# Two gates of the first merge among the last steps of the latent attention, a third ahead of the first branch product, and the splits of the branches' outputs later

## What is computed

```python
o_rwkv = _rwkv7_mix(p_rwkv, ...)
o_mla = _mla_mix(p_mla, ...)          # 8 heads, causal softmax over blocks of 128 queries
o_diff = _diff_mix(p_diff, ...)       # ends in an RMS norm over each head of 128
gates = jax.nn.sigmoid(p_gate + b_gate[l]).reshape(B, S, N_BRANCHES, D_MODEL)
merged = (gates[:, :, 0] * (o_rwkv @ w_branch_rwkv[l])
          + gates[:, :, 1] * (o_mla @ w_branch_mla[l])
          + gates[:, :, 2] * (o_diff @ w_branch_diff[l]))
x = x + merged @ w_o[l]
```

## Time and profile before

| | |
|---|---|
| Median of 3 runs | 3469.41 us (3463.99 to 3471.94) |
| Span of the profiled execution | 3464.9 us; no other time is given for that execution |
| Busy: PE, PEld, DVE, ACT, POOL | 3340.3, 2696.5, 1814.4, 1294.8, 116.1 us |
| Chain that ended last | PE 86%, DVE 8%, ACT 4% |
| Mean granted TensorE clock | 0.989 of full speed |
| End of the latent attention's last matmuls | 547.15 us |
| First merge | from there to about 754 us |

### The profile page before, as it was taken

How to read it: one execution, slowest core, us unless ns; L and a number is a source line. 1 busy time by engine, 2 the same in 40 slices (tenths; PEclk the granted TensorE clock), 3 DMA queues, 4 the chain that set the end, 5 groups by cost and what they waited for, 6 DMA issues and landing times.

```text
span 3464.9 us, 46862 instructions
## 1 busy us (share of the span) xinstructions
PE 3340.3 (96%) x19963; PEld 2696.5 (78%) x19963; DVE 1814.4 (52%) x3053; ACT 1294.8 (37%) x2160; POOL 116.1 (3%) x210
## 2 busy tenths in 40 slices
PE   7999989999999999999899999999999989999998
PEld 5878756888888888887568888888888756788887
DVE  5565664577656665654754533353334475453333
ACT  4232565335434422234543322332223354342222
POOL 0000000010000010100000000000000000000000
PEclk9999999999999999999999999999999999999999
DMA  3110013464444265643112222322333311223231
GB/s 139 39 50 24 31 43 110 161 220 142 153 157 151 90 241 195 244 139 101 32 55 86 97 96 94 98 92 98 97 98 112 105 38 49 86 85 97 98 97 67
DMA packets 100544, 364.08 MB, mean 105 GB/s; under 512 B 11632, under 2 KB 11696, under 8 KB 99696
## 3 DMA queue, kind: packets, MB, share of 16 engines
q1 hardware_dynamic: 75888, 272.14, 23.6%
q0 software_dynamic: 24448, 88.95, 7.8%
HBM read 358.94 MB, written 2.10 MB: 104 GB/s over the span
## 4 chain that ended last, share of the span: by engine, by line
PE 86%; DVE 8%; ACT 4%; issue 1%; DMA 0%; POOL 0%; DVEq 0%; ACTq 0%; POOLq 0%
PE ps_run L435 85%; PE ps_run L781 1%; DVE wl L1890 1%; DVE nrm L1897 1%; ACT nrm L1171 1%; DVE HL L1897 1%; ACT wh L1171 1%; ACT nP L1171 0%; DVE nst L2565 0%; DVE ug L1890 0%; DVE AL L1890 0%; DMA vec<-vec 0%; ACT HH L1171 0%; DVE dP L2258 0%; DVE nrm L1890 0%
## 5 line engine op out<-in xcount | busy, mean ns | idle before, releaser
L435 PE MATMUL ps_run<-HH,wh 128*128 128x512 f32 (+1 forms) x2720 | 1064.8, 391 | 17.8 <-DVE wl L1890 10.5
L435 PE MATMUL ps_run<-HH,wl 128*128 128x512 f32 (+1 forms) x2720 | 1038.4, 382 | 0.0
L435 PE MATMUL ps_run<-HL,wh 128*128 128x512 f32 (+1 forms) x2720 | 1037.8, 382 | 0.0
L1890 DVE TENSOR_TENSOR wl<-st,wh 128x1024 fp32r<-128x1024 f32 x511 | 624.9, 1224 | 733.9 <-ACT wh L1171 733.8
L1171 ACT ACTIVATE wh<-st 128x1024 fp32r<-128x1024 f32 x511 | 537.3, 1054 | 708.4 <-PE ps_run L435 703.4
L435 PEld LDWEIGHTS ps_run<-HH,wh 128*128 128x128 f32 x2720 | 512.9, 189 | 127.5 <-DVE wl L1890 8.5
L435 PEld LDWEIGHTS ps_run<-HL,wh 128*128 128x128 f32 x2720 | 513.5, 189 | 100.0 <-issue 5.5
L435 PEld LDWEIGHTS ps_run<-HH,wl 128*128 128x128 f32 x2720 | 512.8, 189 | 100.1
L435 PE MATMUL ps_run<-AH,wh 128*128 128x512 f32 (+1 forms) x1167 | 443.6, 380 | 2.1 <-DVE wl L1890 2.1
L435 PE MATMUL ps_run<-AH,wl 128*128 128x512 f32 (+1 forms) x1167 | 441.2, 378 | 0.0
L435 PE MATMUL ps_run<-AL,wh 128*128 128x512 f32 (+1 forms) x1167 | 441.2, 378 | 0.0
(11 more groups left out here) (408 smaller groups left out, 3344.2 us busy)
## 6 DMA issues: line engine op xcount, KB each, us to landing
st<-wst SPq DMA_DIRECT2D x511, 512.0 KB, 3.3
mb<-ada POOLq DMA_DIRECT2D x144, 512.0 KB, 4.4
cw<-cw POOLq DMA_DIRECT2D x4, 1024.0 KB, 7.0
X<-xT SPq DMA_DIRECT2D x8, 256.0 KB, 10.2
X<-xT POOLq DMA_DIRECT2D x8, 256.0 KB, 5.1
out<-X SPq DMA_DIRECT2D x8, 256.0 KB, 2.8
kc<-kc POOLq DMA_DIRECT2D x1, 1139.5 KB, 7.4
mb<-cond POOLq DMA_DIRECT2D x2, 512.0 KB, 5.1
```

What stands on the lines that cost most here:

```text
L435: i = self.e.matmul(out, lhsT, rhs, start=start, stop=stop, skip_group_check=True)
L1890: self.e.tensor_tensor(out, a, b, op).then_inc(*self.w.done(*points))
```

## The change

PE: gates 0 and 1 are cut into four pieces each of six matmuls, and two pieces stand behind the work of each of the steps 15, 16, 17 and 18 of the latent attention. Then come gate 2, branch products 0, 1 and 2, and from round 3 on gate and branch product as before.

ACT and DVE: the split that belongs to the first eight blocks stands ahead of the wait for the latent attention. Of the eight splits of branch outputs, four come first. ACT makes the other four in round 1, DVE one in each of the rounds 1 to 4. ACT's Silu moves into round 5. The list `fill` is not touched in rounds 0 to 5, and gives two steps in rounds 6 to 11, one in 12 to 15 and two from 16 on; that is 32 steps, as before.

```diff
-        finish(pipeline(16, (values, both(turn), scores), (4, 3, 0)))
+        ahead = chained(self.first_gate(0, 0), self.first_gate(0, 1))
+        for step, _ in enumerate(pipeline(16, (values, both(turn), scores), (4, 3, 0))):
+            if step >= 15:
+                next(ahead, None)
+                next(ahead, None)
+        finish(ahead)
...
-        gate(*order[0])
-        gate(*order[1])
+        gate(*order[2])
         branch(*order[0])
         branch(*order[1])
-        for this in order[2:]:
+        branch(*order[2])
+        for this in order[3:]:
             gate(*this)
             branch(*this)
...
         order = m.o[0:4] + m.o[8:12] + m.o[4:8]
+        finish(self.spend(8))
         w.wait_ge("dve mla")
         w.wait_ge("pe mla")
         w.own()
-        for j in range(8):
+        for j in range(4):
             self.half(("o", j), order[j], m.AH[j])
-        self.modulation(0)
         for br in range(3):
             for i in range(8):
-                finish(self.spend(8))
                 k = 8 * br + i
+                if k:
+                    finish(self.spend(8))
+                if k == 1:
+                    for j in range(4, 8):
+                        self.half(("o", j), order[j], m.AH[j])
+                if k == 5:
+                    self.modulation(0)
                 w.wait_ge("gate", br, i)
...
+        finish(self.spend(8))
         w.wait_ge("mla out")
         w.wait_ge("pe mla")
-        for j in range(8):
+        for j in range(4):
             self.rest(("o", j), order[j], m.AH[j], m.AL[j])
...
+                if k:
+                    finish(self.spend(8))
                 finish(self.spend(4))
+                if 1 <= k <= 4:
+                    self.rest(("o", 3 + k), order[3 + k], m.AH[3 + k], m.AL[3 + k])
...
-                for _ in range(2 if br == 2 else 1):
+                for _ in range(0 if k < 6 else 1 if 12 <= k < 16 else 2):
                     next(fill, None)
```

More of the change, by code:

```diff
@@ L896, in values, with first_gate @@
                             kt == 0, kt == i, *([("mO", n)] if kt == i else []))
-        finish(pipeline(16, (values, both(turn), scores), (4, 3, 0)))
+        ahead = chained(self.first_gate(0, 0), self.first_gate(0, 1))
[4 more added lines that the diff above has]
+        finish(ahead)
+    def first_gate(self, br, i):
+        m = self.m
+        base = 1792 + 416 + 1536
+        return self.linear(("gate", br, i), fe(c128(base + br * 1024 + i * 128), "w_in", (0,), 8), m.HH, m.HL, None, (0, 1, 2, 3))
     def merge_first(self):
         m = self.m
-        base = 1792 + 416 + 1536
         dense = (0, 1, 2, 3)
@@ L906, in gate @@
         def gate(br, i):
-            finish(self.linear(("gate", br, i), fe(c128(base + br * 1024 + i * 128), "w_in", (0,), 8), m.HH, m.HL, None, dense))
+            finish(self.first_gate(br, i))
         def branch(br, i):
```

## The result

| | us, median (lowest to highest) | runs |
|---|---|---|
| before | 3468.89 (3463.66 to 3472.75) | 20 |
| changed | 3475.14 (3469.90 to 3479.54) | 20 |

The ratio is 1.0019, with a 95% interval of 1.0013 to 1.0025: some 6.6 us slower, between 4.5 and 8.7. The forecast was 1.5 us faster, and the measured time lies above the range that was given. The difference is just under the 0.2% named at the start, but with 20 runs on each side the interval excludes no change. The profiled execution took 3476.05 us, with a span of 3474.1.

A forecast was written before the change was run, and what follows sets the result against it. PE, busy for 96% of the span, was taken as the bound. The terms 9.1 + 2.2 - 3.0 - 3.75 - 0.3 - 2.7 gave +1.5 us gained, so 3469.4 became 3467.9 us, range 3461.5 to 3474.5.

The forecast's parts named there:

- three waits: New PE waits: 3.0 us ahead of gate 2, 3.75 ahead of gate 3, 2.7 at round 5's `dsum`; clock holding.
- rival (3): The clock falls in all three new waits: 8.1 us slower, 3477.5 us; decided at gate 2; chance 0.05.
- Silu term: Round 5: the condition's load and two table loads delay the sigmoid, so PE waits 2.7 us more at `dsum`.
- rival (2): Clock falls in one new wait, likeliest the middle one: 1.6 us or up to twice that, 3470.3 us; chance 0.20.
- The tail: End of the latent attention: gate matmuls between its steps leave no wait and keep the clock up, gaining 9.1 us.
- Rival (4): Clock falls anyway in the latent attention's last steps: sum +9.4 us, 3478.8 us; chance 0.03.
- Slab 3: Old 2.2 us wait at branch product 0 goes; new 3.0 us wait at gate 2; slab 4 just 0.4 us early.
- The bank of gate 3: Gate 3 takes gate 2's bank and waits for that gate's sigmoid: a new PE wait of 3.75 us.
- The marker's sum: Start of gate 3's second half: 4.2 us earlier, from 9.1 + 2.2 - 3.0 - 3.75 less three times 0.1.
- The table loads: On ACT: each costs 1.28 us with the next instruction right behind it, without the 1.38 us drain.
- rival (6): ACT table switches cost up to twice 1.28 us: 1.6 us slower in sum, 3471.0 us; chance 0.02.
- What was moved at no cost: DVE's low parts 4 to 7, the moved `fill` steps and POOL's later `ada` loads cause no new wait.

The follow-up runs named there:

- experiment 3: Changed kernel with ACT splitting slab 3 after step 17 of the latent attention, ahead of the last output's copy; 3473.6 us, ratio 1.0013 to the kernel before.
- Experiment 8: Changed kernel with POOL issuing the three `ada` loads only after the Silu's end; 3475.99 us in one profiled run.
- experiment 4: Changed kernel with gate 2's product in the free bank 6, so gate 3 finds its bank empty; 3469.33 us, ratio 1.0000 to the kernel before.
- experiment 1: Changed kernel with 44 matmuls whose results nobody reads put into PE's three new waits; 3469.02 us, ratio 0.9999 to the kernel before.
- experiment 2: Changed kernel with the Silu in round 9 instead of 5 and `fill` from round 10; 3470.35 us, ratio 1.0002 to the kernel before.
- experiment 5: Changed kernel with gate 2 in bank 6 and the Silu in round 9; 3463.65 us, ratio 0.9983 to the kernel before.
- experiment 6: Changed kernel with gate 2 in bank 6, Silu in round 9, slabs 3 and 4 split in steps 17 and 18; 3461.09 us, ratio 0.9973 to before.

## Why the prediction was wrong

**The clock: the step that failed.** The forecast priced three waits and let the clock hold over each. Its evidence was one row, the wait of 3.02 us ahead of 1183.39 over which it held. It fell behind all three, so the sum lacked a term of 6.1 us: 1.6 behind gate 2, 1.6 behind gate 3, 2.9 behind `dsum` of round 5. The case was there as rival (3), with 0.05. That rival came nearest, 8.1 us slower where 6.6 were measured, but partly by luck: it priced the three falls at 9.6 us instead of 6.1, and its Silu term was 1.9 too small. For the first two falls the lower end of rival (2), 8 matmuls at twice their time, is the right size. Rival (3) also said that it would be decided at gate 2. The falls came together here, but not for that reason: in experiment 3 none comes at gate 2, and the other two come all the same.

The trace of the kernel before held more than that row. In the latent attention the clock was down as soon as PE started again behind a wait of 1.89 us, ahead of 537.75. At two later places with like instructions PE waited 2.8 us, once the clock held and once it fell about 1 us after the restart. PE's timeline of the kernel before at these two places:

```profile
1668.10 1.13 PE L435 MATMUL ps_run<-kw,qT 64*128 64x512 f32 x4 [2.81 <-ACT nP L1171]
...
2809.28 1.13 PE L435 MATMUL ps_run<-kw,qT 64*128 64x512 f32 x4 [2.80 <-ACT nP L1171]
```

And its windows behind the three waits:

```profile
537.00:538.00 1.00, 0.24 (x3) 0.28 (x5) 0.75 (x3) 0.61 (x3) 0.00 (x0) 0.50 0.00 0
1668.10:1672.10 4.00, 4.00 (x28) 2.53 (x29) 3.48 (x10) 3.95 (x7) 0.00 (x0) 1.00 0.30 111
2810.50:2811.50 1.00, 1.00 (x4) 0.81 (x3) 0.82 (x2) 0.98 (x2) 0.00 (x0) 0.50 0.00 0
```

Of the eleven waits of 1.8 to 4.4 us that PE has in that trace (the first, at the kernel's start, left out), seven had the clock at the lower level within 2 us of the restart. Counted like that, a fall behind at least one of the three new waits was the likely case, and not one of 0.25, which rivals (2) and (3) have together.

The rule of the Trainium skill that was weighed against that row, page "TensorE: Matmul & The Clock Gate", section "HAM oscillation — how this bites in real kernels", says that bursts of work with waits between them are throttled again for each burst; its example has waits of some 3 to 5 us. At the three new waits the trace agrees, 3 times in 3. I put it below a single row of the trace. But that row shows one outcome of an event that can go either way. The same wait, 3.01 to 3.03 us long, stands in all ten profiles of this study at the same place. The next 24 matmuls take, from start to start of gate matmuls:

| us | profiles |
|---|---|
| 5.6, the clock held | before, slab 3 early, gate 2 in bank 6, `ada` held |
| 7.1 to 7.2 | Silu in round 9, Silu and bank, before with Silu in round 9 |
| 8.3 to 8.4 | changed, waits filled, Silu bank and slabs |

It held in 4 of 10. Two rows of the changed kernel's timeline of PE, for which the kernel before has 1183.39 and 1188.97:

```profile
1188.08 0.79 PE L435 MATMUL ps_run<-HH,wh 128*128 128x512 f32 x1 [3.03 <-DVE wl L1905]
...
1196.45 0.39 PE L435 MATMUL ps_run<-HH,wh 128*128 128x512 f32 x1
```

That alone puts 2.8 of the 9.2 us between the spans of the two profiles shown. It is most likely chance and no effect of the change, though this can't be told from one profile of each kernel. One and the same kernel does vary that way: in 33 runs of the kernel before, its mean granted clock lies between 0.985 and 0.990, and the two runs at 0.985 took 3471.8 and 3471.9 us, the two at 0.990 3464.1 and 3465.7.

**The Silu: the term that was too small.** The forecast had it start 4.75 us behind POOL's load, which is what the old place showed, and kept 3.5 us as the upper bound for the wait "if POOL's load met more traffic". It started 6.55 us behind (599.31 less 592.76), and D2 came 4.6 us later instead of 2.7. Experiment 8 finds 1.5 of these 1.9: the three loads issued behind it. In the old place the same three loads stood behind it too, and yet it landed in 4.7. That stretch was clear of SP's loads of weights. In experiment 8 SP's loads were there and the three were not, and it took 5.0. So it looks as if both together made it slow; the new place without SP's loads was not tried. The rest of the term is right: two tables and the Silu follow as counted, and `dsum` starts 2.68 us behind the sigmoid, as before (2.69).

**What was right.**
- The tail. Clock 1.00 in all windows from 533.6 to 547.2, no wait in it, and the last values end 19.06 us behind T (548.26 and 1.09, less 530.29), where the forecast's 550.7 less 532.14 is 18.6. Rival (4) is out.
- Slab 3: 2.93 us for 3.0. Experiment 3 shows that slab 4 stood right behind it, as said.
- The bank of gate 3: 3.54 us for 3.75; experiment 4 shows the cause.
- The marker's sum, with the clock up: 4.17 for 4.3 (experiment 1). Changed as it was, T to G3 gained 2.61, since the fall behind gate 2 took 1.6 of it.
- The table loads. The sigmoid at 554.56 starts 0.01 us behind the end of the load of 1.28, and so does the one at 601.68 within 0.02. The drain that the Trainium skill gives, page "ScalarE: Activation LUTs", section "What ACT_TABLE_LOAD costs", isn't there; rival (6) is out.
- What was moved at no cost. D1 to D3 has its old length to 0.02 us as soon as the Silu is out of round 5 (experiments 2, 5, 6), so the low parts and the late `ada` loads cost nothing there. Behind `dsum` of round 5 the changed kernel's PE waits for nothing up to 800, so its `fill` didn't either.

**The sum as it came.** The forecast's +1.5, less 1.9 for the Silu, less 6.1 for the clock, gives 6.5 us slower. The profiles show 6.56, the runs 6.6, with 2 us to either side. That it meets to 0.1 is in part luck, as the terms for the tail, slab 3 and the bank were each off by 0.1 to 0.5.

## What to carry to other kernels

A wait of PE of about 3 us has two prices: its length, and 1.5 to 2.9 us lost in slow work behind it, which it may or may not draw. Count how often such a wait drew it over several profiles before you take one row as proof, and put the chance on the fall. A change that makes one stretch denser but leaves several new short waits behind it loses by them; look for their causes one by one (a bank reused too soon, a split queued behind the last output, a load issued just before it is needed), since each was a few lines' edit here and all of them together turned +0.19% into -0.27%. And try the smallest piece by itself: the Silu moved in the kernel before gave -0.14%, half of that.

## What the runs showed that I had not expected

- Waits of 2.93 us ahead of gate 2 drew the fall in 5 of 5 profiles (one read at 2.92), 3.54 ahead of gate 3 in 4 of 4, 3.06 to 5.17 ahead of `dsum` of round 5 in 4 of 4; 3.02 ahead of 1183 in 6 of 10. Waits of 2.05 and 1.55 (experiment 3) drew none, but the 1.89 ahead of 537.75 did, between short matmuls. So length alone doesn't decide it. What sets apart the 3.02 that holds from the 2.93 that doesn't is open.
- The fall can come late: at gate 3 two matmuls run at full speed behind the wait before the clock goes down.
- The size of the loss varies at one and the same place: 1.5 or 2.7 us ahead of 1183; and from D2 to D3 1.6 (gate 2 in bank 6, `ada` held), 2.3 (slab 3 early) and 2.8 (changed), behind waits of 4.29, 3.06, 5.17 and 4.60, so not in the order of the waits.
- Forty-four matmuls whose results nobody reads made the kernel faster by 6 us: they stand in waits, cost next to nothing there, and the clock stays up.
